# Expert outputs: the two parts of the gated activations interleaved by element, slots 2112 bytes apart

## The reference

```python
q = (xb @ w_pq).reshape(PEER_BLOCK, P_HEADS, 2, P_HALF)
sc = jnp.einsum('thpc,hpkc->thpk', q, sub_keys)
...
g = jax.nn.softmax(fv.astype(jnp.float32), axis=-1).astype(xb.dtype)
ue = jnp.take(u_experts, eid, axis=0)
ve = jnp.take(v_experts, eid, axis=0)
a = jax.nn.gelu(jnp.einsum('thkd,td->thk', ue, xb), approximate=False)
return jnp.einsum('thk,thkd->td', g * a, ve)
```

## Time and profile before

| | |
|---|---|
| median of 2 runs | 2067.55 us (2067.25 to 2067.84) |
| the profiled execution | 2067.93 us |
| its span in the profile | 2066.2 us |
| TensorE busy | 2046.6 us, 99% |
| VectorE, ScalarE, GpSimd busy | 80%, 58%, 17% |
| granted TensorE clock, mean | 0.999 of full |

### The profile page before, as it was taken

How to read it: one execution, slowest core, us unless ns; L and a number is a source line. 1 busy time by engine, 2 the same in 40 slices (tenths; PEclk the granted TensorE clock), 3 DMA queues, 4 the chain that set the end, 5 groups by cost and what they waited for, 6 DMA issues and landing times.

```text
span 2066.2 us, 38366 instructions
## 1 busy us (share of the span) xinstructions
PE 2046.6 (99%) x11544; PEld 1757.1 (85%) x11544; DVE 1658.4 (80%) x3041; ACT 1190.7 (58%) x1901; POOL 346.9 (17%) x342
## 2 busy tenths in 40 slices
PE   8999999999999999999999999999999999999998
PEld 6888888888888888888888888888888898888886
DVE  7786769999998777777688858699999986767676
ACT  6555556667666555555565545566676665555553
POOL 4010110000000433333240101000000004334331
PEclk9999999999999999999999999999999999999999
DMA  6455467776656877777653554577666567777773
GB/s 223 145 164 165 164 201 235 237 232 211 205 193 201 263 242 241 261 241 240 212 185 123 187 179 155 194 237 238 220 221 199 195 212 258 243 241 261 240 242 125
DMA packets 174249, 435.54 MB, mean 211 GB/s; under 512 B 19504, under 2 KB 85040, under 8 KB 173136
## 3 DMA queue, kind: packets, MB, share of 16 engines
q1 hardware_dynamic: 173520, 430.06, 64.0%
q0 software_dynamic: 640, 4.32, 0.6%
HBM read 397.60 MB, written 36.70 MB: 210 GB/s over the span
## 4 chain that ended last, share of the span: by engine, by line
PE 96%; DVE 2%; ACT 1%; DMA 0%; POOL 0%; issue 0%; SPq 0%; DVEq 0%; ACTq 0%
PE ps L1328 35%; PE ps L1709 33%; PE ps L1329 18%; PE ps L1684 3%; PE ps L1600 2%; PE ps L1322 2%; PE ps L1731 1%; PE ps L1625 1%; PE ps L1659 1%; DVE w_lo L845 1%; PE ps L1582 1%; DMA raw<-slabs 0%; PE ps L1498 0%; PE ps L1538 0%; POOL sq L484 0%
## 5 line engine op out<-in xcount | busy, mean ns | idle before, releaser
L845 DVE TENSOR_TENSOR w_lo<-raw,w_hi 128x1024 fp32r<-128x1024 f32 x674 | 838.1, 1244 | 255.6 <-ACT w_hi L790 180.7
L1328 PE MATMUL ps<-act,w_hi 128*128 128x512 f32 x2784 | 985.7, 397 | 0.0
L1329 PE MATMUL ps<-act,w_lo 128*128 128x256 f32 x2784 | 777.6, 279 | 0.0
L1328 PEld LDWEIGHTS ps<-act,w_hi 128*128 128x128 f32 x2784 | 521.7, 187 | 117.2 <-issue 3.0
L1709 PE MATMUL ps<-w_hi,act 128*128 128x512 f32 x1936 | 596.5, 389 | 0.0
L1329 PEld LDWEIGHTS ps<-act,w_lo 128*128 128x128 f32 x2784 | 525.4, 189 | 0.1
L790 ACT ACTIVATE w_hi<-raw 128x1024 fp32r<-128x1024 f32 x248 | 263.1, 1061 | 325.9 <-PE ps L1709 325.9
L1709 PEld LDWEIGHTS ps<-w_hi,act 128*128 128x128 f32 x1936 | 363.4, 188 | 75.5
L1709 PE MATMUL ps<-w_lo,act 128*128 128x512 f32 x968 | 376.6, 389 | 0.0
L521 POOL TENSOR_TENSOR h_in<-h_in,gate 128x256 f32<-128x256 f32 x250 | 243.5, 975 | 436.9 <-DMA h_in<-h_park 436.8
L722 ACT ACTIVATE w_hi<-raw 128x1024 fp32r<-128x1024 f32 x248 | 261.1, 1053 | 0.0
(11 more groups left out here) (261 smaller groups left out, 1829.2 us busy)
## 6 DMA issues: line engine op xcount, KB each, us to landing
raw<-slabs SPq DMA_DIRECT2D x680, 512.0 KB, 4.2
h_park<-h_out SPq DMA_DIRECT2D x256, 128.0 KB, 2.2
h_in<-h_park SPq DMA_DIRECT2D x250, 128.0 KB, 3.8
memT<-mem POOLq DMA_DIRECT2D x2, 1024.0 KB, 6.2
skT<-sub_keys POOLq DMA_DIRECT2D x2, 1024.0 KB, 5.9
x_park<-xT SPq DMA_DIRECT2D x2, 1024.0 KB, 5.9
xT<-x_park SPq DMA_DIRECT2D x2, 1024.0 KB, 7.4
xT<-x SPq DMA_DIRECT2D x4, 256.0 KB, 6.1
```

The source lines that it names most:

```text
L845: nc.vector.tensor_tensor(w_lo[:, j].rearrange("p k c -> p (k c)"), raw[:, j, :], w_hi[:, j].rearrange("p k c -> p (k c)").bitcast(FP32), ...
L1328: nc.tensor.matmul(ps[:, j, :], w_hi[:, j, k, :], a[:, :, k, :], start=(k == 0), stop=False)
L1329: return nc.tensor.matmul(ps[:, j, hi * T:hi * T + T], w_lo[:, j, k, :], a[:, hi, k, :], start=False, stop=(k == KB - 1))
```

## The change

The activations of a slab are kept in one tile, `act_v`, of 4 slots x (256 + 8) tokens x 2 parts. The hi part of a token and its lo part are neighbours, so that the tokens of one part stand 8 bytes apart, and a slot with its gap of 8 token places takes 2112 bytes. ScalarE's copy writes, VectorE's subtraction reads and writes, and TensorE's loads of weights read, with this step. `h_in` and `y_nat` move behind the new tile, and 256 bytes more are taken in each partition, which shifts the constants that follow. The early slabs keep their separate tiles. On every engine the instructions, their order and their waits are those of before; the order of the three parts and of the sums is unchanged.

```diff
--- before.py
+++ after.py
@@ -32,6 +32,7 @@
 
 P = 128
 LINE = 1024
+GAP = 8
 D = 1024
 KB = D // P
 T = 256
@@ -177,8 +178,11 @@
         act_2 = sb("act_2", [P, 2, KB, T], F32R)
         act_hi, act_lo = act_2[:, 0], act_2[:, 1]
 
-        y_nat = [at(f"y_nat{b}", act_at + (2 * b + 1) * RING * T * 4, [P, 2, 512]) for b in range(TB)]
-        h_in = at("h_in", act_at + RING * T * 4, [P, RING, T])
+        act_v = at("act_v", act_at, [P, RING, T + GAP, 2], F32R)[:, :, 0:T, :]
+        h_at = act_at + RING * (T + GAP) * 8
+        top[0] += RING * GAP * 8
+        y_nat = [at(f"y_nat{b}", h_at + b * RING * T * 4, [P, 2, 512]) for b in range(TB)]
+        h_in = at("h_in", h_at, [P, RING, T])
 
         hot_cols = [at(f"hot_col{i}", x_at + i * 1024, [P, 2, P, 2], FP16) for i in range(HOTS)]
         hot_rows_2 = [at(f"hot_row{i}", x_at + 2048 + i * 2048, [P, 2, PARTS, P, 2], FP16) for i in range(HOTS)]
@@ -772,15 +776,20 @@
                     gelu_of(HOT_AT + m // RING * RING, 0, m % RING)
                 assert n == GROUPS
 
-                def gated_hi(g, j, hi=act_hi, h=h_in):
+                def gated_hi(g, j):
 
                     act.wait_ge(gated_ready, layer * V_SLABS + g * RING + j + 1)
-                    nc.scalar.activation(hi[:, j:j + 1, :], h[:, j:j + 1, :], ACT.Copy).then_inc(ga_hi_ready, 1)
+                    nc.scalar.activation(act_v[:, j, :, 0], h_in[:, j, :], ACT.Copy).then_inc(ga_hi_ready, 1)
+
+                def early_gated_hi(j):
+
+                    act.wait_ge(gated_ready, layer * V_SLABS + j + 1)
+                    nc.scalar.activation(early_hi[:, j:j + 1, :], early_in[:, j:j + 1, :], ACT.Copy).then_inc(ga_hi_ready, 1)
 
                 for j in range(RING):
                     gelu_out(TAIL_AT, 0, j)
                     if j < EARLY:
-                        gated_hi(0, j, early_hi, early_in)
+                        early_gated_hi(j)
                     else:
                         gated_hi(0, j)
                 with act.Fori(0, V_SLABS // RING - 1) as g:
@@ -1244,15 +1253,20 @@
                 for j in (2, 3):
                     lo_part(layer, U_AT + TAIL_AT, 0, j)
 
-                def gated_lo(g, j, hi=act_hi, lo=act_lo, h=h_in):
+                def gated_lo(g, j):
                     dve.wait_ge(ga_hi_ready, layer * V_SLABS + g * RING + j + 1)
-                    nc.vector.tensor_tensor(lo[:, j:j + 1, :], h[:, j:j + 1, :], hi[:, j:j + 1, :].bitcast(FP32),
+                    nc.vector.tensor_tensor(act_v[:, j, :, 1], h_in[:, j, :], act_v[:, j, :, 0].bitcast(FP32),
                                             ALU.subtract).then_inc(ga_ready, 1)
+
+                def early_gated_lo(j):
+                    dve.wait_ge(ga_hi_ready, layer * V_SLABS + j + 1)
+                    nc.vector.tensor_tensor(early_lo[:, j:j + 1, :], early_in[:, j:j + 1, :],
+                                            early_hi[:, j:j + 1, :].bitcast(FP32), ALU.subtract).then_inc(ga_ready, 1)
 
                 for j in range(RING):
                     lo_part(layer, V_AT, 0, j)
                     if j < EARLY:
-                        gated_lo(0, j, early_hi, early_lo, early_in)
+                        early_gated_lo(j)
                     else:
                         gated_lo(0, j)
                 with dve.Fori(0, V_SLABS // RING - 1) as g:
@@ -1697,7 +1711,13 @@
 
                 group(layer, U_AT + TAIL_AT, U_EV + TAIL_AT)
 
-                def expert_out(g, j, first=False, final=False, hi=act_hi, lo=act_lo):
+                def tokens(j, b, part):
+                    return act_v[:, j, b * P:(b + 1) * P, part]
+
+                def early_tokens(j, b, part):
+                    return (early_hi, early_lo)[part][:, j, b * P:(b + 1) * P]
+
+                def expert_out(g, j, first=False, final=False, of=tokens):
                     pe.wait_ge(lo_ready[j], lo_count(layer, V_AT, g))
                     pe.wait_ge(ga_ready, layer * V_SLABS + g * RING + j + 1)
                     for half in range(2):
@@ -1705,8 +1725,8 @@
                             if first:
 
                                 pe.wait_ge(act_evac, layer * ACT_EVS + U_EV + RING + TAIL_AT + 2 * b + half + 1)
-                            for i, (w, a) in enumerate(((w_hi, hi), (w_lo, hi), (w_hi, lo))):
-                                last = nc.tensor.matmul(ps[:, 2 * b + half, :], a[:, j, b * P:(b + 1) * P],
+                            for i, (w, part) in enumerate(((w_hi, 0), (w_lo, 0), (w_hi, 1))):
+                                last = nc.tensor.matmul(ps[:, 2 * b + half, :], of(j, b, part),
                                                         w[:, j, 4 * half:4 * half + 4, :].rearrange("p k c -> p (k c)"),
                                                         start=(first and i == 0), stop=(final and i == 2))
                             if final and half + b < 2:
@@ -1714,7 +1734,7 @@
                     last.then_inc(slab_done, 1)
 
                 for j in range(EARLY):
-                    expert_out(0, j, first=(j == 0), hi=early_hi, lo=early_lo)
+                    expert_out(0, j, first=(j == 0), of=early_tokens)
                 expert_out(0, EARLY)
                 with pe.Fori(1, V_SLABS // RING - 1) as g:
                     for j in range(RING):
@@ -1727,8 +1747,8 @@
                             pe.wait_ge(lo_ready[j], lo_count(layer, V_AT, g))
                             pe.wait_ge(ga_ready, layer * V_SLABS + g * RING + j + 1)
                         for b in range(TB):
-                            for i, (w, a) in enumerate(((w_hi, act_hi), (w_lo, act_hi), (w_hi, act_lo))):
-                                last = nc.tensor.matmul(ps[:, 2 * b + half, :], a[:, j, b * P:(b + 1) * P],
+                            for i, (w, part) in enumerate(((w_hi, 0), (w_lo, 0), (w_hi, 1))):
+                                last = nc.tensor.matmul(ps[:, 2 * b + half, :], tokens(j, b, part),
                                                         w[:, j, 4 * half:4 * half + 4, :].rearrange("p k c -> p (k c)"),
                                                         start=False, stop=(j == RING - 1 and i == 2))
                             if j == RING - 1 and half + b < 2:
```

## The result

The changed kernel takes 2082.9 us (median of 2 runs, 2082.79 to 2083.01) against 2067.55 us: 15.35 us more, ratio 1.0075 with a 95% interval of 1.0059 to 1.0091. By the bound of 2% that is no change, but it is clear of the measurement, and the forecast was no change at all, 2063 to 2072 us. Its profiled execution took 2083.01 us, with a span of 2081.3 us.

The account below looks back on a forecast made before the run. TensorE's matmul spacing in the expert-output stage was taken to bound the kernel. All terms were taken as 0: 2067.9 + 0 = 2067.9, against the median 2067.5; forecast no change, 2067.5 us, own range 2063 to 2072, 8-in-10 range 2036 to 2107.

Parts of the forecast that it names:

- What bounds the stage: Expert-output stage: TensorE's unbroken matmul spacing, 226.7 ns, sets the pace; other engines count only if they become slower.
- the value taken for the weight loads, 0: 3000 expert-output weight loads at a step of 8 bytes: no added time, each ns per matmul being worth 3.0 us.
- The bounds, -39 and +39 us: Limits for the stepped weight loads: whole 13.1 ns excess vanishes, or doubles with bytes spanned while the load stays hidden.
- The stepped fp16 load: Line 1684, step of 4 bytes, lasts 97 ns, no longer than contiguous fp32 loads; taken as a reason for no cost.
- the excess that shrinks with 8 columns and moves with timing: Spacing no column accounts for: 7 to 10 ns with 8 weight columns; first ten stage matmuls 229 ns, then 226.7.
- Rival A: Weight loads covering 1024 instead of 512 bytes take more turns from the stream: +10 to +39 us, 2077 to 2107; chance 0.29.
- the 13.1: Expert-output matmuls: ns of the 226.7 ns spacing that no column accounts for, 512 columns costing 213.6 ns.
- the 3 to 6 ns that I read off line 1453: Part of the 13.1 ns excess said to go with the other 120 weight columns, from loads of 8 columns.
- Rival B: Weights and stream advance at equal pace and stop crossing: -10 to -39 us, 2028 to 2058; chance 0.27.
- meetings: Weight load and moving stream sweeping past each other in SBUF, as source of the excess; slots differing in spacing would show it.
- Rival C: A stepped column takes three times as long and the weight load is exposed: +290 us, 2358; chance 0.04.
- Writers, lag and moved tiles: ScalarE's copy (0 to +214 ns), VectorE's subtraction (0 to +277 ns), 5 us slot cover, shifted tiles (0.3 us): all taken as 0.

Follow-up runs that it names:

- e1: Changed kernel without the gap, slots 2048 bytes apart, all loads at position 0, step 8: 2088.37 us, ratio 1.0092.
- e14: Kernel before, plain writers and separate planes, but each load takes every other token, step 8, position 0: 2088.17 us, ratio 1.0090.
- e4: Changed kernel without the gap, each load taking every other token, a step of 16 bytes: 2093.54 us, ratio 1.0116.
- e8: Kernel before with only the activations' two planes 64 bytes further on, streamed weights unmoved, step 4: 2089.96 us, ratio 1.0102.
- e7: Kernel before with everything up to the constants shifted 64 bytes, loads and stream alike: 2069.60 us, ratio 1.0006.
- e13: Changed kernel without the gap, writers still stepped, but loads take 128 neighbouring numbers, step 4, position 0: 2069.49 us, ratio 0.9999.
- e2: Changed kernel with separate planes, step 4, keeping only a gap: slots 1088 bytes apart, positions 0, 64, 128, 192: 2080.29 us, ratio 1.0051.
- e3: Changed kernel without the gap, only the hi part at step 8, lo part in its own plane at step 4: 2088.56 us, ratio 1.0091.
- e5: Changed kernel with separate planes, step 4, slots 1040 bytes apart, positions 0, 16, 32, 48: 2079.67 us, ratio 1.0054.
- e9: Changed kernel with separate planes, step 4, loads at positions 256, 320, 384, 448: 2079.44 us, ratio 1.0057.
- e11: Changed kernel, interleaved at step 8, tile moved 256 bytes on, positions 256, 320, 384, 448: 2083.86 us, ratio 1.0078.

## Why the prediction was wrong

**What bounds the stage** held: only the spacing of the matmuls moved. 3000 matmuls at 5.4 ns make 16.2 us against 15.35 measured, with small changes between the stages.

**The step that failed is the value taken for the weight loads, 0.** In its place the runs showed +5.4 ns a matmul: 6.67 for the step at position 0 (e1, e14), less what the gap gives back. The bounds, -39 and +39 us, held. Both reasons for 0 failed. The stepped fp16 load that I called the nearest row shows how long a load lasts, and length was not the question: a step of 8 adds only 5 or 6 ns to it. And the one spacing "over both parts and over all four slots" was no evidence against a dependence on place: in the kernel before every load starts on a multiple of 512 bytes, so its position, which repeats after 256, was always 0. The row could not have shown otherwise. I had the rows on the other side, the excess that shrinks with 8 columns and moves with timing, and gave them to the rivals.

**Rival A** had the sign, and its lower end (+10 to +19 us) takes in the result: the run of 345.19 us lies in its 342 to 357. That the number fits is partly luck, since it is 20 us of the step less 4 of the gap, which A does not have. Its reason was wrong as a rule. Twice the bytes at position 0 cost 6.67 ns (e1, e14), half of the 13.1 and near the 3 to 6 ns that I read off line 1453; but four times the bytes cost at most 8.3 (e4), and no more bytes at another position cost as much as the step (e8).

**Rival B** was right that the position of the two streams to each other counts (e7, e8), and the sign named for meetings, slots that differ, did show. It was wrong in the direction: at equal pace no position tried was better than the old one.

**Rival C** fell: the load at a step of 8 lasts 194 ns, and even at a step of 16, where it lasts 310, nearly all of it is hidden. **Writers, lag and moved tiles** at 0 held in the sum (e13); ScalarE's own copy became 20 ns longer, out of sight.

Within the changed kernel the two parts of the edit pull against each other. At step 4 the gap alone loses 12 us (e2); at step 8 it wins back about 4 of 20 (e1). What is not settled: why the old arrangement is the best of all tried, why e3 costs as much as e1, how much of e4's 8.3 ns is the load itself, and what meets what inside SBUF. The records show how long loads and matmuls last, not single reads. No arrangement tried beats the kernel before; e7 and e13, its equals, differ from it by nothing that can be told (their intervals take in 1).

## What to carry to other kernels

Where a run of matmuls is unbroken, the addresses of the weights to those of the streamed operand can be part of the price, as in this kernel: look at the spacing of starts, not at durations, and ask what the rows had the chance to vary before taking their constancy for independence. A load that is hidden in time can still slow the stream beside it (e8). To tell a layout's effects apart, move one operand alone and both together: it takes two runs.

## What the runs showed of the hardware

- The spacing of fp32r matmuls over 512 columns depended on the position of the weight load to the streamed operand, and repeated after 256 bytes: 226.7 ns at 0 and 16 bytes, 232.6 to 233.3 at 32 and 48, 233.3 with all slots at 64 (e5, e8; the repeat: e2 against e9, after against e11). At 64 it stayed at 233.3 while no other engine worked (e8).
- A weight load of 128 fp32 columns lasted 188 ns at a step of 4 bytes, 193 at 8, 310 at 16 (e13, e1, e4), while the spacing at position 0 went from 226.7 to 233.3 and 235.0.
- After a change of position the spacing took some matmuls to settle: in slot 0 of e5 four, at about 236, 229, 232 and 231 ns, before 226.7.
